# An encoder layer with expert lookup: 328 instead of 336 dense tokens, and the transfers round the dense stage rearranged

## The reference, cut to what matters

```
q = (xb @ w_query).reshape(TOKEN_BLOCK, PEER_HEADS, 2, PEER_QDIM // 2)
s = einsum("nhpd,hpkd->nhpk", q, sub_keys)            # 128 keys on each of two sides
sv, si = top_k(s, 16)                                 # best 16 of each side
... top_s, eidx = best 16 of the 16 x 16 sums         # 8 heads x 16 = 128 experts a token
g   = softmax(top_s)
hid = gelu(einsum("nd,ned->ne", xb, u_tab[eidx]))     # u_tab: 16384 x 2048, fp32
out = einsum("ne,ned->nd", g * hid, v_tab[eidx])      # v_tab: 16384 x 2048, fp32
```

## Time and profile before

| | |
|---|---|
| median of three executions | 3230.39 us |
| the profiled execution | 3230.31 us |
| its span on the core | 3228.5 us |
| TensorE busy | 3142.5 us (97%) |
| VectorE busy | 2731.9 us (85%) |
| ScalarE, GpSimd busy | 1110.3, 916.1 us |
| granted clock of TensorE, mean | 0.995 |
| DMA, mean over the span | 288 GB/s |

### The profile page before, as it was taken

The page is one execution under the profiler, slowest core; times in us unless marked ns, Lnnn a source line. Parts: engine busy times, 40 slices in busy tenths (PEclk is TensorE's granted clock), DMA queues, the critical chain, the costliest instruction groups (busy, mean ns, idle before and its releaser), DMA issues. The chain is left out here.

```text
span 3228.5 us, 49057 instructions
## 1 busy us (share of the span) xinstructions
PE 3142.5 (97%) x19669; PEld 2985.0 (92%) x19669; DVE 2731.9 (85%) x3943; ACT 1110.3 (34%) x1449; POOL 916.1 (28%) x575
## 2 busy tenths in 40 slices
PE   7999999999999998999999999999999999999998
PEld 3788888888998888989999999999999999999998
DVE  4688888888888999968888888888688888888888
ACT  2223233233224456933333323322332332332333
POOL 2100000002545883022233233333133333233332
PEclk9999999999999999999999999999999999999999
DMA  9844454445547313889999999999799999999997
GB/s 387 317 173 164 165 178 156 179 156 190 206 178 272 127 64 120 232 300 367 370 372 373 370 368 375 371 372 341 305 374 361 363 364 368 372 366 361 369 363 304
DMA packets 175243, 929.09 MB, mean 288 GB/s; under 512 B 16920, under 2 KB 50637, under 8 KB 79949
## 3 DMA queue, kind: packets, MB, share of 16 engines
q1 hardware_dynamic: 123790, 553.15, 46.5%
q0 software_dynamic: 51264, 373.32, 29.6%
HBM read 891.11 MB, written 33.69 MB: 286 GB/s over the span
## 5 line engine op out<-in xcount | busy, mean ns | idle before, releaser
L1624 ACT ACTIVATE sb_raw_hi<-sb_raw_ring 128x2048 fp32r<-128x2048 f32 x256 | 490.9, 1918 | 1123.2 <-DMA sb_raw_ring<-in_v_t 556.3
L1245 PE MATMUL ps_all<-sb_w_hi,sb_raw_hi 128*128 128x336 f32 x2032 | 626.2, 317 | 20.4 <-ACT sb_raw_hi L1624 10.4
L2239 DVE TENSOR_TENSOR sb_raw_lo<-sb_raw_ring,sb_raw_hi 128x2048 fp32r<-128x2048 f32 x256 | 587.9, 2297 | 68.5 <-ACT sb_raw_hi L1624 67.9
L1182 PE MATMUL ps_all<-sb_h_lo,sb_raw_hi 128*128 128x336 f32 x2048 | 637.2, 319 | 0.0
L1182 PE MATMUL ps_all<-sb_h_hi,sb_raw_hi 128*128 128x336 f32 x2016 | 627.8, 318 | 0.7 <-ACT sb_gelu_sb L1631 0.7
L1246 PE MATMUL ps_all<-sb_w_lo,sb_raw_hi 128*128 128x336 f32 x2032 | 624.9, 316 | 0.0
L2600 POOL DMA_INDIRECT sb_gather_ring<-in_u_tab,sb_kept x178 | 281.4, 1581 | 757.7 <-DVE sb_kept L2380 581.2
L2600 POOL DMA_INDIRECT sb_gather_ring<-in_v_tab,sb_kept x178 | 297.6, 1672 | 611.5 <-DVE sb_acc_a L2393 389.4
L1245 PEld LDWEIGHTS ps_all<-sb_w_hi,sb_raw_hi 128*128 128x128 f32 x2032 | 384.2, 189 | 23.4 <-issue 11.8
L1182 PEld LDWEIGHTS ps_all<-sb_h_lo,sb_raw_hi 128*128 128x128 f32 x2048 | 386.6, 189 | 0.0
L1246 PEld LDWEIGHTS ps_all<-sb_w_lo,sb_raw_hi 128*128 128x128 f32 x2032 | 383.9, 189 | 0.0
(11 more groups left out here) (348 smaller groups left out, 5533.9 us busy)
## 6 DMA issues: line engine op xcount, KB each, us to landing
sb_raw_ring<-in_u_t SPq DMA_DIRECT2D x128, 1024.0 KB, 7.8
sb_raw_ring<-in_v_t SPq DMA_DIRECT2D x128, 1024.0 KB, 8.2
sb_arena<-in_ada_wt SPq DMA_DIRECT2D x94, 512.0 KB, 6.0
sb_w_raw<-in_w_t SPq DMA_DIRECT2D x32, 1024.0 KB, 4.9
sb_small<-in_ada_w SPq DMA_DIRECT2D x30, 1024.0 KB, 11.3
sb_w_raw<-in_w_v SPq DMA_DIRECT2D x32, 768.0 KB, 4.3
sb_g_ring<-table_scratch SPq DMA_DIRECT2D x32, 672.0 KB, 8.5
table_scratch<-sb_stage SPq DMA_DIRECT2D x7, 2688.0 KB, 12.3
```

The costliest lines, as they stand in the source:

```text
L1182: last = mm(acc, raw_hi[:, r[0], kk * P:(kk + 1) * P], part, start=i == 0, stop=False)
L1245: mm(accs[c], v, w_hi[:, slots[e], :], start=e == 0, stop=False)
L1624: acti(raw_hi[:, k % 2, :], raw_ring[:, k % RAW, :], ACT.Copy).then_inc(S["un_hi"], 1)
L2239: vec.tensor_tensor(raw_lo[:, k % RAW, :], raw_ring[:, k % RAW, :], raw_hi[:, k % 2, :].bitcast(f32), ALU.subtract)\
```

## The change

- Fourteen "few" tokens instead of six, each on nine partitions with up to fifteen slots. `ND` is 328, `STAGE` 41, `DOTS` 186. The short pieces of route data (L751) are 56 instead of 24.
- The first two loads of `g_ring` come in two parts: seven stages from HBM, the eighth from the stage buffer. The stores of the last stage leave out its first eight blocks, which only these two loads use.
- The rows for the few tokens are repeated in HBM scratch in the query stage, so that the reload is one load of 126 rows.
- The first down unit of every eight multiplies with seven results in both groups of columns, and then waits for the eighth.
- GpSimd's first gather waits for the load of unit 17.

```
-QUARTERS = (0, 16, 48, 88, 128)
+QUARTERS = (8, 16, 48, 88, 128)
-XB = 6
+XB = 14
-STAGE = 42
+STAGE = 41
-        take = carver(placed("kept", M0 + KD * ND + D, [P, 5 * P]))
+        take = carver(placed("kept", M0 + KD * ND + D, [P, 7 * P]))
...
-            sp.dma_start(few_d, o_sb[P - XT - XB:P - XT, NT - 1, :]).then_inc(S["h2x_in"], 16)
+            sp.dma_start(few_d[0:XB, :], o_sb[P - XT - XB:P - XT, NT - 1, :]).then_inc(S["h2x_in"], 16)
...
+                if n == 8:
+                    sp.wait_ge(S["h2x_in"], 16 * (XG + 1))
+                    for j in range(XB):
+                        sp.dma_start(few_d[XB + j * XBP:XB + (j + 1) * XBP, :], few_d[j:j + 1, :].partition_broadcast(XBP)).then_inc(S["row_in"], 16)
...
+            def first_g_load(q):
+                sp.dma_start(g_ring[:, q, 0:NSTAGE - 1, :], g_d[:, q, 0:NSTAGE - 1, :]).then_inc(S[f"g_in{q}"], 16)
+
+            def first_g_copy(q):
+                sp.dma_start(g_ring[:, q, NSTAGE - 1, :], stage[(NSTAGE - 1) % 2][:, QUAD * q:QUAD * (q + 1), :].rearrange("p i c -> p (i c)"))\
+                    .then_inc(S[f"g_in{q}"], 16)
...
-            for n in range(NGROUP):
+            for n in range(NGROUP - 1):
...
-            g_load(0)
-            g_load(1)
+            for q in range(2):
+                first_g_load(q)
+            next_load(EARLY - 3)
+            sp.wait_ge(S["g_ev"], NGROUP)
+            for q in range(2):
+                first_g_copy(q)
+            stage_store(NSTAGE - 1, (0, 1))
             next_load(EARLY - 2)
-            stage_store(NSTAGE - 1, (1, 2, 3))
+            stage_store(NSTAGE - 1, (2, 3))
             g_load(2)
...
                 if k == RELOAD:
                     sp.wait_ge(S["gr_used"], LAST_MIXED + 1)
-                    for j in range(XB):
-                        sp.dma_start(h2x[j * XBP:(j + 1) * XBP, :], few_d[j:j + 1, :].partition_broadcast(XBP)).then_inc(S["h2x_in"], 16)
+                    sp.wait_ge(S["row_in"], 16 * (1 + 2 * GROUPS + XB))
+                    sp.dma_start(h2x[0:XBR, :], few_d[XB:XB + XBR, :]).then_inc(S["h2x_in"], 16)
...
             def down_unit(k, s, g, place, r, slots):
                 wait(pe, "un_hi", k + 1)
-                wait(pe, "w_lo", S8 * s + S8)
+                wait(pe, "w_lo", S8 * s + (S8 if g else S8 - 1))
                 wait(pe, "y_ev", VG * s + g - 1)
                 accs = [bank(4 + 2 * (g % 2) + c)[:, 0:ND] for c in range(2)]
+
+                def high_products(c, e):
+                    v = raw_hi[:, r, e * VW + c * P:e * VW + (c + 1) * P]
+                    mm(accs[c], v, w_hi[:, slots[e], :], start=e == 0, stop=False)
+                    return mm(accs[c], v, w_lo[:, slots[e], :], start=False, stop=False)
+
                 for c in range(2):
-                    for e in range(S8):
-                        v = raw_hi[:, r, e * VW + c * P:e * VW + (c + 1) * P]
-                        mm(accs[c], v, w_hi[:, slots[e], :], start=e == 0, stop=False)
-                        last = mm(accs[c], v, w_lo[:, slots[e], :], start=False, stop=False)
+                    for e in range(S8 if g else S8 - 1):
+                        last = high_products(c, e)
+                if g == 0:
+                    wait(pe, "w_lo", S8 * s + S8)
+                    for c in range(2):
+                        last = high_products(c, S8 - 1)
                 last.then_inc(S["un_half"], 1)
...
-                wait(dve, f"g_in{b // QUAD % 2}", 16 * (b // (2 * QUAD) + 1))
+                wait(dve, f"g_in{b // QUAD % 2}", 16 * (b // (2 * QUAD) + 2))
...
-                    dve.wait_ge(S["h2x_in"], 16 * (XG + 1 + XB))
+                    dve.wait_ge(S["h2x_in"], 16 * (XG + 2))
...
             pool.wait_ge(S["gated"], S8)
+            pool.wait_ge(S[f"un_in{(EARLY + 2) % RAW}"], 16 * ((EARLY + 2) // RAW + 1))
...
-    few_d = nc.dram_tensor("few_scratch", (XB, D), mybir.dt.float32).ap()
+    few_d = nc.dram_tensor("few_scratch", (XB + XBR, D), mybir.dt.float32).ap()
```

## The result

| | before | after |
|---|---|---|
| median | 3230.59 us (4 runs, 3228.35 to 3235.4) | 3212.12 us (4 runs, 3208.36 to 3220.38) |
| ratio | | 0.9949, 95% interval 0.9936 to 0.9962 |
| the profiled execution | 3230.31 us, span 3228.5 | 3220.38 us, span 3218.6 |

The kernel is faster by 18 us; the forecast was 41, and 3212 lies in its range of 3168 to 3220. The profiled execution of the changed kernel is the slowest of its four, so its trace shows 10 of the 18 us.

The account below looks back on a forecast made before the run. The prediction took TensorE's stream of columns as the bound, with DMA close behind. Savings of 22.5 + 2.8 + 7 + 7.5 + 3 = 42.8, less 1.5, gave 41 us: 3230.3 to 3189 us, range 3168 to 3220.

Parts of the forecast that it names:

- 1, the pitch: Dense stage: matmuls of 328 columns take 149.8 ns instead of 153.1, worth 38.9 us if nothing else holds the units.
- 2, sixteen gathers more: Dense stage: DMA at 384 and 382 GB/s gives units of 7.33 and 7.29 us, so 22.5 us of gain.
- rival B: Dense stage: three gather slots lack spare time, late low parts stop TensorE at down units; 3212 us, chance 0.17.
- C: Dense stage: DMA is already full and brings 373 GB/s at most; 3236 us, chance 0.09.
- A: Dense stage: DMA has room for 400 GB/s and more, TensorE keeps its pace; 3173 us, chance 0.28.
- D: Hand-over and reload: the mending saves nothing and TensorE stops elsewhere; 3203 us, chance 0.06.
- The signs of the forecast: Pitch 149.8 ns, DMA 380 to 386 GB/s at 0.98 share, first-group gather waits 45 us, no 4 us stops at mended places.
- 3, the table: Table stage paced by VectorE: one token fewer in each of eight stages' last groups saves 2.8 us.
- 4, the hand-over: From table to dense stage: 7 of 9.2 us lost are saved, less 1.5 us for late first gathers.
- 5, the reload: Reload of the third group's rows: one plain 1 MB load, 2.7 us at 390 GB/s, saves 7.5 us.
- 6, route pieces: Copies on SP before the first table store: 56 take 16.8 us and end at 1267; cost 0, at most 3 us.
- 7, the eighth block late: Down units: the eighth block's product comes 28 matmuls later, giving 4.2 us of cover and saving 3 us.

Follow-up runs that it names:

- the width alone: Kernel before the change with only XB = 14 and STAGE = 41 (328 dense columns, 186 gathers a half), transfers as before: 3232.59 us, ratio 1.0006.
- gates first: Changed kernel with VectorE's low part of block 15 moved behind the eight gates and their low parts: 3211.84 us, ratio 0.9932.
- both reload runs: Changed kernel with the reload reading x1_scratch instead of few_scratch (3216.54 us, one run), or loading 128 rows instead of 126 (3212.32 us, ratio 0.992).
- three mends: Changed kernel with a third pair of PSUM banks, gates ahead of block 15's low part, and a reload of 128 rows: 3192.28 us, ratio 0.9874.
- the third pair alone: Changed kernel with down units turning over three pairs of PSUM banks instead of two, except the last eight: 3199.28 us, ratio 0.9881.
- the edits alone: Changed kernel with 336 dense columns and six few tokens again (XB = 6, STAGE = 42), all other edits kept: 3216.03 us, ratio 0.9944.

## Why the prediction was wrong, point by point

**1, the pitch: right.** 200 us / 1335 = 149.8 ns, the figure forecast; 1327 in the changed kernel's best window.

**2, sixteen gathers more: the step that failed.** It took 384 and 382 GB/s as steady rates, and so 7.33 and 7.29 us a unit and 22.5 us of gain. In the profiled execution the first half has 7.33 and the second 7.46; four other traces with 328 columns and two pairs of banks (the width alone, gates first, both reload runs) have 7.32 to 7.39 in the first and 7.34 to 7.41 in the second. By the times, the width is worth nothing alone (1.0006), nothing beside the edits (0.9944 to 0.9949) and 9 to 11 us beside three mends that the change doesn't have. The rates weren't wrong: 383 GB/s over 600 us in the changed kernel's first half, and 390 with TensorE nearly at full pace in the three mends. Wrong was that a mean rate sets the time. With 0.6 us to spare for a gather slot, as I had worked out, VectorE waits up to 3.8 us for one of its large gathers, it takes everything in order, and what it does next is wanted by TensorE. I had priced the ring's lack of slack at nothing in the sum, and put it into rival B. What the runs show is where TensorE pays: the third pair alone gives 13 to 22 us. Why VectorE is late they don't settle. Shorter gathers and shorter work on VectorE help alike, and no run has a fourth gather slot, so that the ring's depth is the cause is argued, not shown.

**Rival B** has the time, 3212, and nearly the mechanism: VectorE's waits for gathers grew (44.1 us from 25.2), TensorE stopped at down units, the clock fell. Where it named late low parts, the wait was mostly for the addition that frees a PSUM pair (18.7 us against 2.4 for blocks' low parts and 2.5 for results'); the third pair showed it. Its number is in part luck, since the 16 us that it took from parts 3 to 7 came from other places than it said. C is out as a mechanism: 368 GB/s at a share of 0.94 with 5 us of stops isn't a full DMA. A is out for this kernel, though by the prediction 389 GB/s would have been enough, and the three mends have 390 in the first half. D has a good part of the truth: hand-over and reload together save 4.3 us, not 14.5.

The signs of the forecast came mixed. The pitch is there and the wait for gathers is just short of its 45 us. The rates are 383 and 373 GB/s at shares of 0.96 and 0.95 instead of 0.98, and behind the reload a stop of 4.81 us stands, with the clock at 0.83 from 2180 to 2200 us.

**3, the table: right, but for a slip.** VectorE's last low part begins at 1376.83 instead of 1378.23, and the first store at 1268.20 instead of 1267.49: 2.1 us, forecast 2.8. With 0.26 us a token, as worked out there, one token takes 0.59 us and not 0.5, and eight stages save 2.1.

**4, the hand-over: mis-sized.** Forecast 7 saved less 1.5. The edits alone save 23 matmuls in the first window, 3.5 us; with the width 2.5 us (9.4 to 6.9). The stop at unit 17 went, as said. The stop at unit 15 grew to 4.81 us from 3.25: I had seen that the low part of block 15 stands ahead of the gates, and called it "some 2 us". It was nearly the whole of what was left, as the gates-first run shows: 332 of 334 matmuls.

**5, the reload: mis-sized.** Forecast 7.5 saved; 4.0 with 336 columns, 1.8 with 328 against the kernel before. "One plain load, 2.7 us at 390 GB/s" was the error: a load of 126 rows held all DMA at 271 GB/s for 11 us, as the six of 21 rows had at 248. "DMA: Bandwidth & Descriptors" of the Trainium skill, section "Why a DMA increments its semaphore by 16 and not by 1", says that a transfer runs on the largest number of engines up to 16 that divides the outermost dimension of both its sides. Worked out by that rule, an estimate, it is 14 for 126 rows, 7 for 21, 9 for 9, and 16 for 128. No run counts the engines; the rates with 126 and 128 rows, 271 and 414 GB/s, go the same way. Why the other traffic slows down too, no run here shows. The prediction left the rule out; it speaks for 126 rows over 21, and for 128 over both.

**6, route pieces: right.** 56 pieces took 16.77 us, the first table store is at 1268.20, not past 1270.

**7, the eighth block late: under-sized.** Forecast 3 us. In the three mends it is worth 14 to 18. In the changed kernel 11.0 of the 18.7 us of waits for the addition stand at the third down unit of eight; that the edit without the third pair moved lateness there from the first is likely, but no run undoes it alone.

**The sum of 4 to 7** was 16 us and the edits alone gave 16 by the medians (11.4 by the profiled executions). That is luck, two errors that cancel: 7.5 us in the two windows, not 13, and the rest elsewhere. The trace before had 7.9 us of small waits outside both places (6.7 less 1.5 under "issue", 2.0 and 0.7 of two other kinds), of which I had counted 3.

## What to carry to other kernels

When a bound is lowered and the next two engines stand at 90% and 97%, don't price the gain by their mean rates: ask how much slack each ring and each order has for one late arrival, and where TensorE would wait for it. A buffer at that wait (here two idle PSUM banks) was worth more than the smaller work. And look at what stands first in an engine's order behind a wait: work that nobody needs yet cost a stop of 4.8 us.

## What the runs showed of the hardware that I had not expected

- A 1 MB load of 126 partitions held all DMA traffic at 271 GB/s for 11 us, one of 128 partitions left it at 414. From another source it was as slow (293 over 12 us, one run), at another target 300 GB/s for 6 us, and in a kernel with 336 columns 316 over 12 us.
- DMA gave 390 GB/s over 600 us with gathers and block loads mixed, at a share of 0.97, with TensorE at 3987 of 4005 matmuls.
- A stop of TensorE of 3.17 us was followed by 3.4 us at half clock with 14 matmuls instead of 22 or 23, 1.3 us more. A stop of 2.61 us that ended at 2561.90 was not: from 2562 to 2567 us the clock stands at 1.00. Windows without a stop (1303 and 1335 matmuls in 200 us) stand at 1.00.
